# Regrouping the first layer's modulation: groups of 256 channels, with four gate blocks and the channel transforms inside

## The reference, cut to what matters

```python
shift, scale, gate = jnp.split(sc @ ada_w[0] + ada_b[0], 3, axis=-1)          # and the same of sc_ctx
hx = _rmsnorm(x, norm_g[0]) * (1.0 + scale[:, None]) + shift[:, None]
hc = _rmsnorm(ctx, norm_g[0]) * (1.0 + scale_c) + shift_c
y = (_fourier_mix(h) * jax.nn.silu(h @ w_gate)) @ w_out                       # h is hx, hc
x = x + gate * y

def _fourier_mix(h):      # over tokens, and over the channels within each of 4 groups of 512
    hg = h.reshape(B, T, 4, 512)
    return jnp.fft.fft2(hg, axes=(1, 3), norm='ortho').real.reshape(B, T, D)
```

## Time and profile before

| | us |
|---|---|
| median of 3 runs (lowest, highest) | 3239.34 (3236.70, 3239.69) |
| the profiled execution, its own time | 3236.72 |
| its span in the trace | 3235.0 |
| PE busy | 3128.0 (97%) |
| DVE busy | 2118.6 (65%) |
| ACT busy | 1301.8 (40%) |
| DMA, mean over the span | 201 GB/s |

### The profile page before, as it was taken

One profiled execution on the slowest core, in us unless ns is written; L12 is line 12 of the kernel. 1 busy time (PEld: TensorE's weight loads), 2 busy tenths in 40 slices (PEclk: granted clock), 3 DMA queues, 4 the chain that ended last, 5 costly groups with the idle time before them and its releaser, 6 DMA issues.

```text
span 3235.0 us, 44077 instructions
## 1 busy us (share of the span) xinstructions
PE 3128.0 (97%) x17440; PEld 2617.6 (81%) x17440; DVE 2118.6 (65%) x3651; ACT 1301.8 (40%) x2056; POOL 163.6 (5%) x252
## 2 busy tenths in 40 slices
PE   7899999999999999999999999999999999989998
PEld 4677777878888888878777889899899988968776
DVE  2377654687887855666568855555756566556897
ACT  3322322522232222232445554444444344435676
POOL 0100000100000000000100000001100200010001
PEclk8999999999999999999999999999999999989999
DMA  8757685344545445467357736456664433666897
GB/s 298 281 189 271 242 285 203 104 166 155 195 167 177 167 158 191 157 201 238 126 200 253 244 120 197 135 172 200 208 209 146 144 118 127 198 247 202 293 370 273
DMA packets 190718, 648.91 MB, mean 201 GB/s; under 512 B 21920, under 2 KB 30240, under 8 KB 190128
## 3 DMA queue, kind: packets, MB, share of 16 engines
q1 hardware_dynamic: 136016, 450.96, 40.5%
q10 hardware_dynamic: 49536, 178.28, 16.2%
q0 software_dynamic: 4960, 16.85, 1.5%
HBM read 628.19 MB, written 15.73 MB: 199 GB/s over the span
## 4 chain that ended last, share of the span: by engine, by line
PE 84%; DVE 7%; ACT 4%; DMA 2%; issue 1%; POOL 0%; ACTq 0%; SPq 0%; POOLq 0%; DVEq 0%
PE PS L466 13%; PE PS L468 13%; PE PS L467 13%; PE PS L563 6%; PE PS L565 6%; PE PS L564 6%; DVE WL L1926 3%; ACT WH L1271 2%; PE PS L1169 2%; PE PS L808 2%; DMA AR<-ada_p 2%; PE PS L1171 2%; PE PS L1170 2%; PE PS L643 1%; PE PS L866 1%
## 5 line engine op out<-in xcount | busy, mean ns | idle before, releaser
L1926 DVE TENSOR_TENSOR WL<-WR,WH 128x1024 fp32r<-128x1024 f32 (+1 forms) x644 | 779.9, 1217 | 552.9 <-ACT WH L1271 550.0
L1271 ACT ACTIVATE WH<-WR 128x1024 fp32r<-128x1024 f32 (+1 forms) x644 | 672.9, 1051 | 951.3 <-PE PS L468 574.4
L466 PE MATMUL PS<-HTH,WH 128*128 128x256 f32 (+1 forms) x2624 | 871.2, 332 | 0.3 <-DVE WL L1926 0.3
L468 PE MATMUL PS<-HTH,WL 128*128 128x256 f32 (+1 forms) x2624 | 857.7, 327 | 0.0
L467 PE MATMUL PS<-HTL,WH 128*128 128x256 f32 (+1 forms) x2624 | 857.5, 327 | 0.0
L466 PEld LDWEIGHTS PS<-HTH,WH 128*128 128x128 f32 x2624 | 499.7, 190 | 61.6 <-issue 14.8
L467 PEld LDWEIGHTS PS<-HTL,WH 128*128 128x128 f32 x2624 | 499.8, 190 | 42.9 <-issue 1.7
L468 PEld LDWEIGHTS PS<-HTH,WL 128*128 128x128 f32 x2624 | 499.7, 190 | 42.8
L563 PE MATMUL PS<-WH,HTH 128*128 128x512 f32 x1016 | 408.2, 402 | 3.6 <-DVE WL L1926 3.6
L565 PE MATMUL PS<-WH,HTL 128*128 128x512 f32 x1016 | 396.3, 390 | 0.0
L564 PE MATMUL PS<-WL,HTH 128*128 128x512 f32 x1016 | 395.6, 389 | 0.0
(11 more groups left out here) (419 smaller groups left out, 4027.5 us busy)
## 6 DMA issues: line engine op xcount, KB each, us to landing
WR<-ada_w SPq DMA_DIRECT2D x256, 512.0 KB, 4.6
AR<-ada_p SPq DMA_DIRECT2D x128, 512.0 KB, 6.6
WR<-m_vo ACTq DMA_DIRECT2D x64, 512.0 KB, 4.2
WR<-a_qz ACTq DMA_DIRECT2D x64, 512.0 KB, 4.7
WR<-n_m SPq DMA_DIRECT2D x64, 512.0 KB, 4.2
WR<-e_gu SPq DMA_DIRECT2D x53, 512.0 KB, 5.3
YT<-e_gu SPq DMA_DIRECT2D x51, 512.0 KB, 5.6
WR<-f_out ACTq DMA_DIRECT2D x32, 512.0 KB, 5.3
```

The costliest lines, as they stand in the source:

```text
L466: e.matmul(ps[:, 0:n], wh[:, k, :], xh, start=c == 0, stop=False)
L468: i = e.matmul(ps[:, 0:n], wl[:, k, :], xh, start=False, stop=c == K - 1)
L1271: e.activation(WH[:, s % NP, 0:n_], place_of(plan["slot"][p])[:, 0:n_], ACT.Copy, scale=1.0).then_inc(*L.up(hi_done, ("hi", s)))
L1926: e.tensor_tensor(WL[:, s % NP, 0:n_], place_of(plan["slot"][plan["split"][s]])[:, 0:n_], WH[:, s % NP, 0:n_].bitcast(F32), ALU.subtract). ...
```

## The change

Layer 0's first stage is rebuilt around groups of 256 channels (`GP` = 8 shares). Four gate blocks (`NG0` = 4) and the transforms are accumulated in it, in units u = 0 to 7 of two blocks each; the other twelve gate blocks follow in the order by hand. Banks 0 to 3 hold the gates, 4 and 5 a half transform (two of the four token blocks), 6 and 7 the shares. The pieces of the gate chunks are 256 KB and take turns in two halves of WH's third place; the two transform pieces stay in the first two places for the whole stage. The eight shares of the next unit run on PE in one go (`some_shares(8)`). The squares are summed by DVE, so PE needs only 8 + 8 small products for the statistics, and the reciprocal is taken of 4 columns before they are spread. All low parts of h are made by DVE; POOL has no part in layer 0. `transformed` is called twice a group. In the later part of layer 0 the `bg` half blocks are placed anew: 22 beside gates, 3 beside mixes, 24 beside outputs, and the gate vector of layer 0 is finished in two halves.

```diff
-NG0 = 6
-GP = 16
+NG0 = 4
+GP = 8
@@ F_ORDER(0)
-            return [*(("dft", g) for g in range(4)), ("mix", 0), ("mul", 0), ("mul", 1), ("gate", 6), ...
+            return [("mix", 0), *(("mul", n) for n in range(4)), ("gate", 4), ("gate", 5), ("mix", 1), ...
@@ where the pieces lie
-        LATER[place_] = range(64 + at, 64 + at + (3 if k < 20 else 2))
+        LATER[place_] = range(64 + at, 64 + at + (3 if k < 16 else 2))
+    GATES0 = [0, 1, 2, *range(5, 18)]
+    DFT0 = (3, 4)
+    def ws(s):
+        return DFT0.index(s) if s in DFT0 else 2 if s < 18 else (s + 2) % NP
+    def users_before(s):
+        if s in GATES0:
+            c = GATES0.index(s)
+            return [GATES0[c - 2]] if c > 1 else []
+        return [] if s < 18 else GATES0[14:16] if s == 18 else [DFT0[s - 19]] if s < 21 else [s - NP]
@@ PE, first_gates
+            def chunk(c, n, turned=None):       # 12 matmuls
...
+            def transform(g, p, n, turned=None):   # 24 matmuls, token blocks 2p and 2p + 1
...
+            shares(0, range(4), side(0))
+            sums_of("x0", 512)
+            shares(0, range(4, 6), side(0))
+            rows_from("x0", 512)
+            shares(0, range(6, 8), side(0))
+            turn_share(0, side(0))
+            for u in range(8):
+                g = (u - 1) // 2
+                left += [(u + 1, m) for m in range(8)] if u < 7 else []
+                if u == 0:
+                    chunk(0, 0)
+                    chunk(1, 0)
+                    some_shares(8)
+                    turn_share(1, side(1))
+                elif u % 2:
+                    chunk(2 * u, 0)
+                    transform(g, 0, 0)
+                    some_shares(8)
+                    chunk(2 * u + 1, 0)
+                    if u == 7:
+                        transform(3, 1, 0)
+                else:
+                    transform(g, 1, 0, u)
+                    some_shares(8)
+                    chunk(2 * u, 0, u + 1)
+                    chunk(2 * u + 1, 0)
@@ ACT, first_norm
+            root("x0", 512)
+            cut_to(2)
+            w.wait_ge(L.at(("full", ("rs", "x0"))))
+            e.activation(RS, place[("rs", "x0")][:], ACT.Copy, scale=1.0)...
+            for u in range(8):
+                adap_row(u)
+                if u % 2 and u > 1:
+                    transformed(0, (u - 3) // 2, (2, 3), 1)
+                ...                              # the four high parts of blocks 2u and 2u + 1
+                cut_to(GATES0[2 * u + 1] + 1)
+                if u % 2:
+                    transformed(0, (u - 1) // 2, (0, 1), 0)
+            for n in range(NG0):
+                gate(("gate", 0, n), ...)
+            cut_to(19)
+            transformed(0, 3, (2, 3), 1)
+            cut_to(18 + NP)
@@ DVE, first_norm
+            for u in range(8):
+                mod_of(u)
+                ...                              # four scaled halves, the low parts two behind
+                cut_to(GATES0[2 * u] + 1)
+                for x in late:
+                    low(*x)
+                late.clear()
+                cut_to(GATES0[2 * u + 1] + 1)
@@ DVE, square_sum, and outproject
+        for n in range(NB - 1):
+            square_sum("x0", n)
-                some = {0: 1, 1: 2 + n % 2}.get(tag, 0) if n < 14 else 0
+                some = {0: 2 if n < 10 else 1, 1: 2 + n % 2}.get(tag, 0) if n < 14 else 0
@@ POOL
-        modnorm(0, ALL)
```

More of the change, by code:

```diff
@@ L570, in statistics, with sums_of @@
         def statistics(tag, n):
+            sums_of(tag, n)
+            rows_from(tag, n)
+        def sums_of(tag, n):
             ps = wrk(("stat", tag))
[L572 to L577, removed]
             r = RS if n == 512 else RA
@@ L657, in side, with some_shares @@
                 return lambda job: bank(6 + c % 2, job)
[L659 to L669, removed]
+            gates = [bank(n, ("gate", 0, n)) for n in range(NG0)]
+            weights(("first", 0), [I["f_gate0"][c] for c in range(3)])
+            weights(("dft", 0), halves(I["dft_d"]))
+            weights(("first", 0), [I["f_gate0"][c] for c in range(3, NB)])
+            left = []
+            def some_shares(n):
+                for _ in range(n):
+                    if left:
+                        c, m = left.pop(0)
+                        shares(c, [m], side(c))
+            def chunk(c, n, turned=None):
+                s = GATES0[c]
+                wh, wl = part_of(WH, s), part_of(WL, s)
                 w.wait_ge(L.at(("lo", s), ("h", 0, c)))
[L671 to L674, removed]
+                for k, ps in enumerate(gates):
+                    b = slice(128 * k, 128 * k + 128)
                     e.matmul(ps[:], wh[:, b], HH_[:, c, :], start=c == 0, stop=False)
@@ L677, in first_gates @@
                     i = e.matmul(ps[:], wl[:, b], HH_[:, c, :], start=False, stop=c == 15)
-                    names = ([("full", ("gate", 0, n))] if c == 15 else []) + ([("used", s)] if n == NG0 - 1 else [])
+                    names = ([("full", ("gate", 0, k))] if c == 15 else []) + (
+                        [("used", s)] if k == NG0 - 1 else [])
                     if names:
                         i.then_inc(*L.up(mm_done, *names))
-                if at < GC - 1 and more:
-                    shares(g + 1, range(*parts[at + 1]), side(g + 1))
@@ L1398, in fnet @@
             tbs = list(range(a0 // 128, b0 // 128))
[L1399 removed]
             if tag == 0:
[L1401 to L1403 removed]
+                first_norm()
+            else:
+                modnorm(tag, before, cols, free)
             for kind, n in F_ORDER(tag):
@@ L2148, in fnet @@
                 w.wait_ge(L.at(("xst", 2)))
-            else:
-                for n in range(NG0):
-                    gate(("gate", 0, n), f_z(0, n), F_TMP[n % 2], ("gated", 0, n))
             def apart(g):
```

193 lines of the change are left out of this document (116 added, 77 removed).

## The result

The kernel with the change takes 3262.05 us (median; 3259.17 to 3265.37) against 3238.73 us (3236.70 to 3239.69) for the kernel before in the same series: ratio 1.0074, 95% interval 1.0061 to 1.0087. It is slower, by 23.3 us. The forecast, 3240.5 in 3228 to 3254, was wrong. The profiled execution took 3261.14 us for a span of 3259.4, against the span of 3235.0 before: 24.4 us more.

What follows compares the result with a forecast made beforehand. PE bounds the kernel from the transforms' end; earlier, stages short of data and of PE alternate. The stage ends at 192.8 us, 19.7 sooner; with +21.9 and -1.0 that makes +1.2: 3240.5 us, range 3228 to 3254.

Steps and rivals of the forecast that it cites:

- Part 7: Behind the stage: mix -1.0 us, first later share 0, second `bg` beside output blocks nothing, DMA bounds 0 and 3 us.
- (d): Rival: output blocks run short of DMA, +3 us and as much again if SP's queue delays `reload`: 3246; chance 0.05.
- Part 3: PE's work in the stage (chunks, half transforms, shares 8 to 63, seven turns): 117.2 us that nothing can hide.
- Part 6: Low clock in the stage: two stretches at the start and 4 of 7 bursts, 9.0 us, bounds 3 and 13.5.
- Part 2: Start of the stage: first chunk at 41 us, between 38 and 44, against 61.8 before.
- Part 4: Seven bursts of eight shares on six buffers: PE idles 18.9 us in all, between 11 and 33.
- Part 5: PE's waits for h in the stage: 5.2 us in unit 1, 1.5 in units 3, 5 and 7 together.
- (b): Rival: every burst turns the clock down and slows its last shares, +12.9 us, 3253; chance 0.24.
- Part 1: Two gate blocks, 96 matmuls, leave the stage with its transforms and come back later at full price: +21.9 us.
- Behind layer 0: Planner and smaller groups in layer 1: nothing on the path.
- The signs I had named: Profile checks: chunk 0 at 41 us, fourteen burst waits, last transform at 193; wrong if PE idles beside gate and output blocks.
- The chance of 0.27 for slower: Whole kernel slower by over 0.2%: (b) and half of (d) together, 0.27.

Runs made afterwards that it cites:

- e2: Changed kernel with the shares for output block n + 1 ahead of block n's second `bg` half block on SP's queue: 3254.29 us, ratio 1.0049.
- e5: e4 with the first three shares of layer 1 ordered ahead of the half block beside the first mix: 3231.34 us, ratio 0.9979.
- e8: Changed kernel, bursts kept, with eight buffers for the shares instead of six: 3234.21 us, ratio 0.9986.
- e10: e8 with the queue orders of e2 and e5 added: 3219.56 us, ratio 0.9947.
- e1: Changed kernel with one `bg` half block instead of two beside each of the first ten output blocks: 3253.93 us, ratio 1.0044.
- e12: The kernel before the change with eight buffers for the shares and nothing else: 3230.83 us, ratio 0.9978.
- e4: Changed kernel with the edits of both e2 and e3: 3235.27 us, ratio 0.9987.
- e3: Changed kernel with each unit's eight shares spread over its chunks and half transforms, one or two at a time: 3243.52 us, ratio 1.0022.

## Why the prediction was wrong, by its own steps

**Part 7, the step that failed.** Two of its sentences did. "Output blocks now carry two `bg` for n < 10" ended in "nothing", since I priced the second `bg` by DVE's time (2.5 us on 6.4 of 11) and by bytes (384 GB/s; measured 290 to 300). Both sums were sound, and both were the wrong question. What the second `bg` adds is a wait on SP's queue, behind which the share loads of the next block stand. "The first later share is late as before: 0" failed alike: DVE now has two cuts between the mix and its `bg`, the order for the shares comes at 205.47 us, 9.8 us behind the mix's start where it was 7.9, and the chain shows 9.13 us to landing at 206.34, then PE's waits. In numbers: PE waits 10.1 us instead of 0.8 behind the stage, 9.3 of the 14.8. The granted clock, which before stayed at 1.00 there, fell twice behind these waits:

```profile
215.46:218.87 3.41, 3.36 (x14) 2.07 (x15) 1.42 (x2) 0.00 (x0) 0.00 (x0) 0.50 0.81 287
410.00:416.86 6.86, 5.96 (x20) 4.09 (x21) 2.92 (x6) 0.00 (x0) 0.00 (x0) 0.50 1.03 405
```

Half of PE's 9.3 busy microseconds in these two windows is 4.7 us, which with the waits is 14.0 of the 14.8. By the runs, the order beside the outputs is worth 7.8 us (e2) and the first late share 3.9 (e5). My rival (d) had the place, and half a sentence on SP's queue, but had the queue delay `reload` and not the shares, and priced the whole at 6 us, half of it by bandwidth, with a chance of 0.05. The queue was the mechanism, bandwidth was none. The -1.0 for the mix came as some -0.8: in the trace before PE waits 0.78 us ahead of it, in the one after not at all.

**Part 3, a term mis-sized.** "Together 117.2 us that nothing can hide" left out what PE pays when it turns from full matmuls to shares and back. In the stage there are 155.1 us from chunk 0 to the last transform (40.33 to 195.42), of which 17.3 are waits for shares and 5.3 waits for h: 15.3 remain above 117.2, where Part 6 gave 9.0 to the clock. Of the 6.3 that are missing, seven bursts at 0.31 are 2.2, and the clock is 3.8 (see Part 6).

**Part 2**: right. 41 us forecast, 40.33 measured.

**Part 4**: right, but it should have been a warning. Fourteen waits were forecast at 18.9 us, and 14 came with 17.3; the first burst lasts 6.9 us (48.10 to 55.05). I took the price of six buffers for eight shares as part of the change, and never asked what the bursts would be without it. e8 gives 27.8 us for that, 10 more than the waits themselves.

**Part 5**: nearly right, 5.2 forecast in unit 1, 4.41 and 0.50 measured; the units behind were less late than I had them (5.3 in all against 6.7).

**Part 6**: right in its count, too low in its price. With the one at unit 1 counted as a stretch of the start, the clock fell behind four of the seven bursts. But PE was busy for 25.6 us at a clock of 0.50 between chunk 0 and the first mix, which by the halving above cost 12.8 us and not 9.0, near the upper bound of 13.5. In e8, whose bursts don't wait, it is 4.7. Rival (b), every burst, is thus refuted in the stage, though its total of 3253 stands nearer to the result than mine; a total can be near for another reason.

**Part 1**: right, as far as the runs show it. In e10, where PE waits for nearly no share, the first mix to the end of layer 0 takes 367.6 us; the 344.6 of before and 21.9 for 96 matmuls make 366.5. No run took the two blocks out alone.

**Behind layer 0** I gave 0, and 5.3 us came. The other kernels, whose program there is the same as the changed one's (but for e1, which moves ten half blocks there), took 2677.4 to 2681.2 us from the milestone on, e12, with the order of before, 2680.1, before itself 2677.1, after 2682.4. The division by idle and clock tells more. At full clock PE's work there is 2577.9 to 2578.4 us in all fourteen traces. PE idles 74.2 us before and 75.8 after (75.0 to 76.3 in all kernels made from the changed one, 74.3 in e12), and the low clock takes 24.9 us before and 28.7 after, by the same halving. So 3.8 of the 5.3 are the clock, which took 27.9 us in e12 too, whose program there is that of before: that part differs from execution to execution. Some 1.6 us of idle time may belong to the change; no run tried it.

**The signs I had named** served well: "PE idles beside the gate and output blocks" was the one that came true. The chance of 0.27 for slower was fair, but the kernel is slower by another way than the one that it rested on: the clock cost 3.8 us more than forecast in the stage, not the 12.9 of (b). The range was not fair, because it took in the bounds of terms that I had found, and had no room for one of the 15 us kind that I had priced at nothing.

## What to carry to other kernels

When work is added to an in-order queue, list what stands behind its wait, and when that was issued before; a load that used to go out 0.7 us after its buffer came free is worth more than the bytes it shares DMA with. A burst of transfers that is longer than its ring of buffers pays at every burst, and takes away what an overlay could win; try ring and overlay together, since in this kernel of bursts each alone gave nothing that shows (3262.1 and 3259.2 against 3259.3 us) and both together 25 us. Keep small matmuls of another shape together: here one insertion cost what two thirds of a share cost. When a loss doesn't add up from waits, count PE's busy time at the low clock as well.

## What the runs showed of the hardware

- A share of eight 128x32 by 256 matmuls between full matmuls of 128x128 by 512 costs 0.31 us beyond its own 0.48 (e4, 2.16 us for a period of 1.37 and 0.48). In a whole burst a share is 0.45 (e8). I had no price for this, and it made whole bursts better than spreading: the stage of e8 is 11.1 us shorter than that of e3.
- A burst with two waits turns the clock down in some places and in others not (waits of 1.41 and 1.49 us kept it at 1.00, waits of 1.40 and 1.45 us did not), and the same code in another execution differs: 0.94 and 0.89 over 84 to 114 us in the kernel after and in e2.
- In fourteen traces PE's work behind layer 0, with idle time and half of the busy time at a granted clock of 0.50 taken out, is 2577.9 to 2578.4 us, while the stretch as a whole takes 2677.1 to 2682.4.
